# Two unused pads move TensorE's moving buffers by 32 bytes in SBUF

## The chip, the core and the metric

The kernel runs on one core of one Trainium2 chip, as a single launch. The metric is the device time of one execution in microseconds (us); lower is better. All weights and activations are float32.

## What is computed

The reference is two transformer stacks in a row on 256 tokens of width 1024. The first has two layers, each FFN, mixer, FFN; the second has one layer, mixer and FFN. Every FFN is a SwiGLU of inner width 2816, and makes up most of the work:

```python
def swiglu(h, w_gate, w_up, w_down):
    return (jax.nn.silu(h @ w_gate) * (h @ w_up)) @ w_down

for layer in range(DEPTH):                       # DEPTH = 2
    x = x + 0.5 * swiglu(rms_norm(x, ffn1_norm[layer]), ...)
    h = rms_norm(x, mix_norm[layer])
    x = x + even_mixer(h, ...)  if layer % 2 == 0 else  x + odd_mixer(h, ...)
    x = x + 0.5 * swiglu(rms_norm(x, ffn2_norm[layer]), ...)
x = rms_norm(x, final_norm)
...
# second block, one layer, 16 meta tokens ahead of the 256
h = h + concat([mla_mixer, diff_mixer, swa_mixer]) @ w_out
h = h + (silu(hn @ w_gate) * (hn @ w_up)) @ w_down
```

The mixers are attentions (a global and a windowed one, a neighbourhood one, and three kinds in the second block), each with an input projection and an output projection.

## The kernel before, in words

**The weights.** All large weight matrices pass through a ring of six slots, one block of 128 x 1024 numbers in each. SyncE loads a block into `w_raw` (`load`). ScalarE rounds it to the float32r format in `w_hi` (line 914), and VectorE writes the rest, `w_raw - w_hi`, to `w_lo` (line 1371). The activations are split in the same way. A product is then three matmuls at full rate: high with high, high with low, low with high.

**The transposed activations.** `act_t` holds the normed activations with the feature on the partition: for each of 8 feature tiles k, 256 columns of high parts and 256 of low parts. ScalarE writes the high parts (line 935), VectorE the low ones (line 1412), at each norm. `hid_t` holds three tiles of the FFN's inner activations in the same form (ScalarE at line 992, VectorE at line 1525). `out_t` and `hid_t`, and the last three tiles of `act_t`, hold the attention outputs for the output projections (`out_pair`).

**The matmuls.** A matmul has a stationary operand, loaded by LDWEIGHTS, and a moving operand, which streams past it. Each matmul here has a weight load of its own. The page prints the moving operand first in the list of inputs: `gu<-sb_act_t,sb_w_hi` has `act_t` moving and a 128 x 128 piece of `w_hi` stationary.

- `gate_up` (line 2054), first tiles in `first_tile` (2021) and `opening_tile` (2031, 2035): `act_t` moves, 512 columns (high and low at once) against `w_hi`, then 256 against `w_lo`.
- `cols_block` (line 2066) and `last_cols` (line 2108): the down product of the first four FFNs. `hid_t` moves, 256 columns, in groups of three: `w_hi`, `w_hi`, `w_lo`.
- `half_block` (line 2089) and again `last_cols` (2108): the output projections. `hid_t`, `out_t` and tiles of `act_t` move, 256 columns each, by the same code.
- the chunks at lines 2294, 2439 and 2557: queries and keys, `act_t` moves, 256 columns.
- the other projections (lines 2232, 2263, 2523) and the down product of the last FFN (2127, 2134, 2146): the weights move and `act_t` or `hid_t` is stationary.

The stretch that the change touches is the list of buffers; the order in which these calls get their memory sets the addresses:

```python
        w_raw = sb("w_raw", [P, RING, BLK])
        w_hi = sb("w_hi", [P, RING, BLK], F32R)
        w_lo = sb("w_lo", [P, RING, BLK], F32R)

        act_t = sb("act_t", [P, KT, 2 * SEQ], F32R)
        meta_t = sb("meta_t", [P, KT * 4 * META + META], F32R)
        hid_t = sb("hid_t", [P, 3, 2, SEQ], F32R)
        out_t = sb("out_t", [P, 2, 2 * SEQ], F32R)
        x = sb("x", [P, KT, SEQ])
```

and the two places that most matmuls come from are

```python
                            ins = nc.tensor.matmul(gu[:, b, w, 0:width], part[:, s, cols], act_t[:, k, 0:width],
                                                   start=(k == 0 and i == 0), stop=(k == KT - 1 and i == 1))
```

```python
                        for i, (part, rhs) in enumerate(((w_hi, rhs_hi), (w_hi, rhs_lo), (w_lo, rhs_hi))):
                            ins = nc.tensor.matmul(y[:, b, c * SEQ:(c + 1) * SEQ], part[:, s, cols], rhs,
                                                   start=(first and c == 0 and i == 0), stop=False, skip_group_check=True)
```

**Addresses.** The buffers lie one behind the other in each partition. In the built program `w_raw` starts at byte 16512, and the sizes in the list give the rest. What matters below is the address modulo 128 bytes, called the phase here. All offsets inside `w_hi`, `w_lo` and `act_t` that matmuls use are multiples of 128 bytes, and those inside `hid_t` and `out_t` are multiples of 1024, so each buffer has one phase:

| buffer | byte before | phase before | byte after | phase after |
|---|---|---|---|---|
| w_raw, w_hi, w_lo | 16512, 41088, 65664 | 0 | the same | 0 |
| act_t | 90240 | 0 | 90272 | 32 |
| meta_t | 106624 | 0 | 106656 | 32 |
| hid_t | 108736 | 64 | 108768 | 96 |
| out_t | 114880 | 64 | 114912 | 96 |
| x and all that follows | 118976 | 64 (x) | 119104 | the same as before |

Of the kernel before, what the change touches and what calls it, by code (L numbers as in the profile page):

```python
# [21 lines left out]
P = 128  # L22
# [261 lines left out]
def build(nc, a, out):  # L284

    ctx = ExitStack()
    with ctx:
        def sb(name, shape, dt=F32):
            return ctx.enter_context(nc.sbuf_tensor("sb_" + name, shape, dt))
# [6 lines left out]
        w_hi = sb("w_hi", [P, RING, BLK], F32R)  # L296
        w_lo = sb("w_lo", [P, RING, BLK], F32R)

        act_t = sb("act_t", [P, KT, 2 * SEQ], F32R)
        meta_t = sb("meta_t", [P, KT * 4 * META + META], F32R)  # L300
        hid_t = sb("hid_t", [P, 3, 2, SEQ], F32R)
        out_t = sb("out_t", [P, 2, 2 * SEQ], F32R)
        x = sb("x", [P, KT, SEQ])
        work = sb("work", [P, TT, WORK])
        mwork = sb("mwork", [P, MWORK])
# [2493 lines left out]
```

## Time and profile before

| | |
|---|---|
| median of 3 runs | 1295.4 us (1294.29 to 1295.53) |
| the profiled execution | span 1298.1 us; no other time is recorded for it |
| TensorE matmul busy | 1274.0 us, 98% of the span |
| VectorE, ScalarE, GpSimd busy | 77%, 57%, 11% |
| mean DMA rate | 180 GB/s |
| mean granted TensorE clock | 0.996 |

The span runs from the first to the last instruction. It is 2.7 us over the median of the timed runs. Matmuls overlap each other in the profile, since each is shown with its way through the array; the pace is read from their starts.

### The profile page before, as it was taken

The page shows a single profiled execution, that of the slowest core. Times are in us where ns is not written, and L with a number is a line of the kernel's source. Part 1 is how long each engine was busy: PE and PEld are TensorE (multiplying, and loading weights), DVE is VectorE, ACT ScalarE, POOL GpSimd, SP SyncE. Part 2 cuts the span into 40 slices and gives each one's busy share as a digit, 9 for nine tenths or more (in the row PEclk, how much of TensorE's full clock was granted, in tenths as well). Part 3 has the DMA queues.
Part 4 walks back from the last instruction along what each step waited for, and adds up shares of the span by engine and source line. Part 5 has one row for each costly group of instructions (what it writes and reads, how often), then busy time and mean ns, then how long its engine had stood idle before and what let it go on. Part 6 is the DMA issues. An engine that isn't in the chain of part 4 may idle for free.

```text
span 1298.1 us, 24356 instructions
## 1 busy us (share of the span) xinstructions
PE 1274.0 (98%) x8455; PEld 1135.3 (87%) x8455; DVE 994.7 (77%) x1863; ACT 736.5 (57%) x1331; POOL 142.1 (11%) x229
## 2 busy tenths in 40 slices
PE   7999999999999999999999999999999999999997
PEld 6899999788899998999988889999998868888886
DVE  6877778968887778777786758877777677877775
ACT  6555556766555556555555556555556655655553
POOL 5000003202330000000002202000005410000000
PEclk9999999999999999999999999999999989999999
DMA  9866655537996647665649537666657412666650
GB/s 283 258 186 193 184 188 147 154 117 198 268 258 189 194 147 219 185 185 186 194 141 263 171 108 231 213 184 188 194 153 183 134 46 82 204 185 193 183 172 33
DMA packets 295612, 233.57 MB, mean 180 GB/s; under 512 B 13180, under 2 KB 270532, under 8 KB 295552
## 3 DMA queue, kind: packets, MB, share of 16 engines
q1 hardware_dynamic: 288432, 213.80, 55.2%
q0 software_dynamic: 6688, 18.60, 5.8%
q8 instruction: 38, 0.62, 0.2%
q10 hardware_dynamic: 432, 0.36, 0.1%
q14 instruction: 22, 0.18, 0.1%
HBM read 229.79 MB, written 7.55 MB: 183 GB/s over the span
## 4 chain that ended last, share of the span: by engine, by line
PE 89%; DVE 5%; DMA 2%; ACT 2%; issue 1%; POOL 0%; SPq 0%; POOLq 0%; DVEq 0%; ACTq 0%
PE gu L2054 42%; PE y L2066 16%; PE y L2146 4%; PE gu L2439 4%; PE y L2108 3%; PE gu L2263 2%; PE y L2089 2%; PE gu L2089 2%; PE gu L2232 2%; DVE sb_w_lo L1371 2%; PE gu L2021 1%; DMA sb_w_raw<-in_ffn_w_up 1%; PE y L2477 1%; PE gu L2454 1%; PE y L2466 1%; PE gu L2294 1%
## 5 line engine op out<-in xcount | busy, mean ns | idle before, releaser
L2054 PE MATMUL gu<-sb_act_t,sb_w_hi 128*128 128x512 f32 x1680 | 587.9, 394 | 0.0
L1371 DVE TENSOR_TENSOR sb_w_lo<-sb_w_raw,sb_w_hi 128x1024 fp32r<-128x1024 f32 (+1 forms) x405 | 496.0, 1229 | 89.8 <-ACT sb_w_hi L914 83.5
L914 ACT ACTIVATE sb_w_hi<-sb_w_raw 128x1024 fp32r<-128x1024 f32 (+1 forms) x405 | 423.9, 1052 | 70.8 <-PE y L2066 30.7
L2054 PE MATMUL gu<-sb_act_t,sb_w_lo 128*128 128x256 f32 x1680 | 434.7, 279 | 0.0
L2054 PEld LDWEIGHTS gu<-sb_act_t,sb_w_hi 128*128 128x128 f32 x1680 | 307.4, 188 | 55.3
L2054 PEld LDWEIGHTS gu<-sb_act_t,sb_w_lo 128*128 128x128 f32 x1680 | 316.1, 188 | 14.9
L2066 PE MATMUL y<-sb_hid_t,sb_w_hi 128*128 128x256 f32 x1216 | 218.7, 280 | 3.5 <-DVE sb_hid_t L1525 3.5
L980 ACT ACTIVATE sb_work<-gu 128x256 f32<-128x256 f32 x220 | 84.0, 382 | 237.1 <-PE gu L2054 230.8
L2066 PEld LDWEIGHTS y<-sb_hid_t,sb_w_hi 128*128 128x128 f32 x1216 | 190.5, 188 | 7.8 <-DVE sb_w_lo L1371 2.9
L2066 PE MATMUL y<-sb_hid_t,sb_w_lo 128*128 128x256 f32 x608 | 170.2, 280 | 0.0
L1504 DVE TENSOR_TENSOR sb_work<-gu,sb_work 128x256 f32<-128x256 f32 x220 | 92.6, 423 | 96.4 <-ACT sb_work L980 96.4
L2066 PEld LDWEIGHTS y<-sb_hid_t,sb_w_lo 128*128 128x128 f32 x608 | 114.1, 188 | 0.0
L1508 DVE TENSOR_TENSOR sb_work<-sb_work 128x256 f32<-128x256 f32 x220 | 94.5, 431 | 8.4 <-ACT sb_work L1001 1.2
L992 ACT ACTIVATE sb_hid_t<-sb_work 128x256 fp32r<-128x256 f32 x110 | 46.0, 418 | 80.3 <-DVE sb_work L1519 80.3
L643 POOL TENSOR_TENSOR sb_small<-sb_small 128x2 f32<-128x2 f32 (+3 forms) x16 | 19.4, 1212 | 465.9 <-DVE sb_small L1459 461.7
L985 ACT ACTIVATE sb_work<-sb_work 128x256 f32<-128x256 f32 x110 | 46.0, 418 | 24.5 <-DVE sb_work L1508 24.0
L1519 DVE SCALAR_TENSOR_TENSOR sb_work<-sb_work 128x256 f32<-128x256 f32 x110 | 47.0, 427 | 11.1
L1525 DVE TENSOR_TENSOR sb_hid_t<-sb_work,sb_hid_t 128x256 fp32r<-128x256 f32 x110 | 46.8, 425 | 5.3 <-ACT sb_hid_t L992 5.3
L1060 ACT ACTIVATE sb_prob<-sb_prob,sb_small 128x256 f32<-128x256 f32 (+1 forms) x88 | 42.0, 482 | 14.9 <-DVE sb_small L1810 10.4
L1513 DVE SCALAR_TENSOR_TENSOR sb_work<-sb_work 128x256 f32<-128x256 f32 x110 | 46.7, 425 | 3.2 <-ACT sb_work L985 2.4
L1074 ACT ACTIVATE sb_prob_t<-y 128x512 f32<-128x512 f32 (+1 forms) x42 | 23.2, 587 | 45.3 <-PE y L2466 33.2
L2439 PE MATMUL gu<-sb_act_t,sb_w_hi 128*128 128x256 f32 x256 | 47.6, 287 | 0.0
(357 smaller groups left out, 1649.4 us busy)
## 6 DMA issues: line engine op xcount, KB each, us to landing
sb_w_raw<-in_ffn_w_gate SPq DMA_DIRECT2D x88, 512.0 KB, 3.8
sb_w_raw<-in_ffn_w_up SPq DMA_DIRECT2D x88, 512.0 KB, 3.7
sb_w_raw<-in_ffn_w_down SPq DMA_DIRECT2D x88, 512.0 KB, 3.3
sb_w_raw<-in_odd_w_qkv SPq DMA_DIRECT2D x24, 512.0 KB, 6.6
sb_w_raw<-in_w_gate SPq DMA_DIRECT2D x22, 512.0 KB, 3.8
sb_w_raw<-in_w_up SPq DMA_DIRECT2D x22, 512.0 KB, 3.7
sb_w_raw<-in_w_down SPq DMA_DIRECT2D x22, 512.0 KB, 3.6
sb_w_raw<-in_even_w_in SPq DMA_DIRECT2D x12, 512.0 KB, 3.8
```

What stands on the lines that cost most here:

```text
L914: nc.scalar.activation(w_hi[:, slot, 0:w], w_raw[:, slot, 0:w], ACT.Copy).then_inc(hi_done, 1)
L980: nc.scalar.activation(halves[:, b, w, :], gu[:, b, w, SEQ:2 * SEQ], ACT.Copy).then_inc(half_copied, 1)
L1371: nc.vector.tensor_tensor(w_lo[:, slot, 0:w], w_raw[:, slot, 0:w], w_hi[:, slot, 0:w].bitcast(F32), ALU.subtract).then_inc(lo_done, 1)
L1504: nc.vector.tensor_tensor(sums[:, b, w, :], gu[:, b, w, 0:SEQ], halves[:, b, w, :], ALU.add).then_inc(gu_summed, 1)
L1508: nc.vector.tensor_tensor(sums[:, b, w, :], sums[:, b, w, :], rstd_row, ALU.mult).then_inc(scaled, 1)
L1519: nc.vector.scalar_tensor_tensor(out=hidden[:, b, :], in0=gated[:, b, :], scalar=0.5, in1=sums[:, b, 1, :], op0=ALU.mult, op1=ALU.mult).th ...
L1525: nc.vector.tensor_tensor(hid_t[:, h, 1, :], hidden[:, b, :], hid_t[:, h, 0, :].bitcast(F32), ALU.subtract).then_inc(hidden_split, 1)
L2054: ins = nc.tensor.matmul(gu[:, b, w, 0:width], part[:, s, cols], act_t[:, k, 0:width], start=(k == 0 and i == 0), stop=(k == KT - 1 and i ...
L2066: ins = nc.tensor.matmul(y[:, b, c * SEQ:(c + 1) * SEQ], part[:, s, cols], rhs, start=(first and c == 0 and i == 0), stop=False, skip_grou ...
L2089: ins = nc.tensor.matmul(mixed(kind, b)[:, c * SEQ:(c + 1) * SEQ], part[:, s, cols], rhs, start=(at == 0 and c == 0 and i == 0), stop=Fals ...
L2146: ins = nc.tensor.matmul(y[:, 2 * t + h, :], lhs[:, tok], part[:, s, h * 512:(h + 1) * 512], start=False, stop=False, skip_group_check=True)
L2439: ins = nc.tensor.matmul(gu[:, c % 2, 1, 0:SEQ], part[:, s, cols], rhs, start=(k == 0 and i == 0), stop=(k == KT - 1 and i == 2))
```

## The change

Two tensors that nothing reads or writes are allocated: 32 bytes per partition ahead of `act_t`, and 96 bytes behind `out_t`. `act_t`, `meta_t`, `hid_t` and `out_t` move up by 32 bytes; everything behind them moves up by 128 bytes, and so keeps its address modulo 128. The weights stay. Every instruction is the same, in the same order and with the same waits; only line numbers grow, by 1 from `act_t` on and by 2 from `x` on (line 2054 becomes 2056).

```diff
         w_hi = sb("w_hi", [P, RING, BLK], F32R)
         w_lo = sb("w_lo", [P, RING, BLK], F32R)
 
+        phase_a = sb("phase_a", [P, 8])
         act_t = sb("act_t", [P, KT, 2 * SEQ], F32R)
         meta_t = sb("meta_t", [P, KT * 4 * META + META], F32R)
         hid_t = sb("hid_t", [P, 3, 2, SEQ], F32R)
         out_t = sb("out_t", [P, 2, 2 * SEQ], F32R)
+        phase_b = sb("phase_b", [P, 24])
         x = sb("x", [P, KT, SEQ])
         work = sb("work", [P, TT, WORK])
         mwork = sb("mwork", [P, MWORK])
```

## Rows read from the trace of the kernel before

**Rows 1.** The page: span, busy time by engine, clock granted in 40 slices.

```profile
span 1298.1 us, 24356 instructions
PE 1274.0 (98%) x8455; PEld 1135.3 (87%) x8455; DVE 994.7 (77%) x1863; ACT 736.5 (57%) x1331; POOL 142.1 (11%) x229
...
PEclk9999999999999999999999999999999989999999
```

**Rows 2.** Waits of PE: who was waited for, us in total, times, longest.

```profile
PE gu L1981 <- DMA sb_gain_rows<-in_ffn_norm: 5.8, 1, 5.8
PE y L2066 <- DVE sb_hid_t L1525: 3.5, 3, 1.2
```

**Rows 3.** Groups of PE by shape: count, then busy us, mean ns, idle before.

```profile
L2054 PE MATMUL gu<-sb_act_t,sb_w_hi 128*128 128x512 f32 x1680 | 587.9, 394 | 0.0
L2054 PE MATMUL gu<-sb_act_t,sb_w_lo 128*128 128x256 f32 x1680 | 434.7, 279 | 0.0
L2066 PE MATMUL y<-sb_hid_t,sb_w_hi 128*128 128x256 f32 x1216 | 218.7, 280 | 3.5 <-DVE sb_hid_t L1525 3.5
L2066 PE MATMUL y<-sb_hid_t,sb_w_lo 128*128 128x256 f32 x608 | 170.2, 280 | 0.0
L2439 PE MATMUL gu<-sb_act_t,sb_w_hi 128*128 128x256 f32 x256 | 47.6, 287 | 0.0
```

**Rows 4.** Line 2108 alone, four stretches: length, PE busy (count), PEld, clock, DMA share.

```profile
191.07:199.55 8.48, 8.48 (x72) 8.43 (x71) 1.00 0.55 161
288.08:293.84 5.76, 5.76 (x48) 5.72 (x48) 1.00 1.01 308
473.85:482.33 8.48, 8.48 (x72) 8.43 (x71) 1.00 0.44 137
780.46:786.22 5.76, 5.76 (x48) 5.72 (x48) 1.00 1.07 311
```

**Rows 5.** Line 2108: duration ns min/median/max by operand.

```profile
L2108 PEld LDWEIGHTS y<-sb_hid_t,sb_w_hi x192: 187/188/189, 190.8 to 971.7; 128*128 128x128 f32 x192
L2108 PE MATMUL y<-sb_hid_t,sb_w_hi x192: 278/279/280, 191.1 to 971.8; 128*128 128x256 f32 x192
...
L2108 PEld LDWEIGHTS y<-sb_act_t,sb_w_hi x48: 192/192/192, 290.8 to 1102.1; 128*128 128x128 f32 x48
L2108 PE MATMUL y<-sb_act_t,sb_w_hi x48: 283/283/283, 291.0 to 1102.2; 128*128 128x256 f32 x48
```

**Rows 6.** Line 2066 alone, in a stretch of full DMA.

```profile
314.41:317.24 2.83, 2.83 (x24) 2.78 (x23) 1.00 1.00 288
```

**Rows 7.** Timeline of PE in a gate and up product: start us, us.

```profile
312.67 0.39 PE L2054 MATMUL gu<-sb_act_t,sb_w_hi 128*128 128x512 f32 x1
312.90 0.28 PE L2054 MATMUL gu<-sb_act_t,sb_w_lo 128*128 128x256 f32 x1
...
313.71 0.39 PE L2054 MATMUL gu<-sb_act_t,sb_w_hi 128*128 128x512 f32 x1
```

**Rows 8.** Timeline of PE, the moving operand a weight: line 2232, then 2146.

```profile
669.61 0.62 PE L2232 MATMUL gu<-sb_w_hi,sb_act_t 128*128 128x512 f32 x2
...
674.38 0.61 PE L2232 MATMUL gu<-sb_w_hi,sb_act_t 128*128 128x512 f32 x2
...
1141.62 0.63 PE L2146 MATMUL y<-sb_w_hi,sb_hid_t 128*128 128x512 f32 x2
1142.09 0.63 PE L2146 MATMUL y<-sb_w_lo,sb_hid_t 128*128 128x512 f32 x2
1142.56 0.39 PE L2146 MATMUL y<-sb_w_hi,sb_hid_t 128*128 128x512 f32 x1
```

**Rows 9.** Line 2414 alone, matmuls of 256 columns of plain float32.

```profile
1048.94:1051.95 3.01, 3.01 (x15) 2.47 (x13) 1.00 0.61 180
```

**Rows 10.** Stretches, all engines: PE, PEld, DVE, ACT, POOL, clock, DMA share, GB/s.

```profile
300.00:360.00 60.00, 57.76 (x381) 52.31 (x381) 49.09 (x77) 32.51 (x54) 21.84 (x30) 1.00 0.98 257
640.00:700.00 60.00, 60.00 (x375) 53.95 (x373) 42.03 (x62) 34.04 (x51) 6.29 (x9) 1.00 0.69 184
```

## The prediction

> **What bounds the kernel now.** I read the page first. TensorE's matmuls are busy for 1274.0 of 1298.1 us, and its clock is at full rate in all slices but one, which is just under [rows 1]. Then the waits of PE: the largest are 5.8 us at the very start and 3.5 us in three pieces [rows 2]. So the kernel is a queue of 8455 matmuls on one engine, and the time is their number times the pace at which they start. A change of pace goes into the time almost one to one. The groups say which matmuls count: 3360 at line 2054 with `act_t` moving and 1824 at line 2066 with `hid_t` moving [rows 3].
>
> Next I asked what the pace is made of. The granted clock of 1.00 is 2.4 GHz, so 256 columns at one a cycle take 106.7 ns and 512 take 213.3. In the gate and up product three pairs of 512 and 256 columns start between 312.67 and 313.71, which is 347 ns a pair against 320.0 [rows 7]: 27 ns too much, or 13.3 a matmul. That excess does not grow with the width: with weights moving, 21 matmuls of 512 columns start between 669.61 and 674.38, 227 ns each, 13.8 over 213.3 [rows 8]. It is a fixed price per matmul, paid nearly everywhere.
>
> **Is an address able to change it?** The trace holds an experiment on this by itself. Line 2108 is one piece of code, run with `hid_t` moving (phase 64) and with `act_t` moving (phase 0); the weights are at phase 0 in both. With `hid_t` 72 matmuls take 8.48 us, 117.8 ns each; with `act_t` 48 take 5.76 us, 120.0 each; and each repeats to the digit elsewhere in the program [rows 4]. The instructions themselves are shorter, 279 against 283 ns, and their weight loads 188 against 192, with hardly any spread [rows 5]. The `act_t` stretches fall where the DMA queues are full, 1.01 and 1.07 against 0.55 and 0.44, so I looked for `hid_t` under full DMA: at line 2066, with a share of 1.00, 24 matmuls take 2.83 us, 117.9 each [rows 6]. DMA is not the cause. What is left that differs is the address of the moving operand. A second pair goes the other way: with the weights moving at phase 0, a stationary `act_t` (phase 0) gives 227 ns, and a stationary `hid_t` (phase 64) gives four starts in 0.94 us, 235 ns [rows 8]. These two lines also differ in the order of their outputs, so that is weaker. I conclude that the phase counts, by 2 to 8 ns a matmul, and that no row shows phase 32 or 96.
>
> **The change part by part.** The pads cost no instruction. Nothing is added to any queue, no wait appears, and no order moves.
>
> 1. *`act_t` moving, phase 0 to 32.* The matmuls are 3360 at line 2054, 160 in the first tiles, 384 at 2439, 192 at 2557, 120 at 2294, and 216 in the output projections: 4432 (where no row is shown, the code gives the count: at line 2557 8 chunks of 8 feature tiles by 3). Unknown price. From below (a gain): the whole excess but that of line 2414, where 14 matmuls start in 3.01 us, 215 ns each for 256 columns of plain float32 [rows 9]; at two cycles a column that is 213.3, so 1.7 ns is left as excess, and the gain could be 11.6 ns each. From above (a loss): the 8 ns of [rows 8]. Between these I take the nearest row, the same line with a moving operand off phase 0 [rows 4]: 120.0 to 117.8, a gain of 2.2 ns. 4432 x 2.2 = 9.8 us.
> 2. *`hid_t` and `out_t` moving, phase 64 to 96.* 1824 at line 2066, 288 at 2108, 360 at 2089: 2472. These are off phase 0 before and after. I take 117.8 ns for both, a change of 0. The bounds: back to 120.0 costs 2472 x 2.2 = 5.4 us; down to 1.7 of excess gains 9.4 ns each, 23 us.
> 3. *`act_t` and `hid_t` stationary, to 32 and 96.* 336 and 264 matmuls. Bounds: minus 264 x 8 = 2.1 us if `hid_t` leaves what makes 235, plus 336 x 8 = 2.7 us if `act_t` enters it. I take 0.
> 4. *Writers of the moved buffers, and everything behind them.* ScalarE and VectorE are at 57 and 77% [rows 1]; a few ns on a write are covered by matmuls in flight. What lies behind keeps its phase. 0. If the cover is gone the engine waits as in rows 2, a few us.
> 5. *What a faster TensorE meets.* In the stretch from 300 to 360 us the DMA share is 0.98 and PE already idles for 2.2 us; in the stretch from 640 it does not idle at all and the share is 0.69 [rows 10]. In the first a gain is given back: 381 of 8455 matmuls, 4.5% of 9.8, is 0.4 us. Next late would be the weight blocks there.
>
> Sum: -9.8 + 0 + 0 + 0.4 = -9.4 us. Against the profiled span that is 1298.1 to 1288.7; the median lies 2.7 below that span, so 1295.4 - 9.4 = 1286.0 us.
>
> The Trainium skill, page "TensorE: Matmul & The Clock Gate", section "Back-to-back issue gap", gives a warm gap of N/2.4 plus 2.5 ns. The plain float32 row comes near that rule and the float32r rows do not. By the rule as a floor that both phases reach, the sum would be near the larger-gain rival below.
>
> **The rivals.**
>
> *A larger gain.* The excess is a clash of two streams that start together from addresses of equal phase, and the new phases take most of it away. For: plain float32 shows that this engine can run with 1.7 ns. Against: phase 64 against 0 was already a different phase, and cured only a sixth. All of it would give -4432 x 11.6 - 2472 x 9.4 = -75 us, 1221; a third of it 1271.
>
> *No change.* The step from phase 0 to 64 helps, but 32 behaves as 0 and 96 as 64, because the memory is organised in pieces of 64 bytes or the buffers differ by something else. 1295.4.
>
> The Trainium skill, page "SBUF — State Buffer", section "Specifications (TRN2)", puts the line of SBUF at 16 bytes. Phases 0, 32, 64 and 96 all begin such a line, so by that rule alone the time would stay. Rows 4 show two such starts that differ, so the rule is not all there is.
>
> *Slower.* A start at 32 or 96 lies across a boundary of 64 bytes, while 0 and 64 lie on one. Every touched stream then reads one piece more. A row gives the size such an effect can have, 8 ns [rows 8]: 6904 moving matmuls x 8 = 55 us, 1351. If only the small difference appears and on the wrong buffers, 2472 x 2.2 = 5.4 us, 1300.8. It decides from 0.4 ns a matmul on: 6904 x 0.38 = 2.6 us. For: no row shows a start off 64 bytes. Against: the two phases that I can see do not rank the way a simple alignment would have it, since 64 is faster than 0.
>
> **How the numbers follow.** A measurement of this kernel can tell 0.2%, 2.6 us, from no change. The forecast (a gain of 2.6 to 20 us) gets 0.37, with its own range of 1276 to 1292; a larger gain 0.15; no change 0.13; slower 0.35, most of it up to 1322 (4 ns on each moving matmul is 27 us) and 0.13 beyond. So faster is 0.52, same 0.13, slower 0.35. The range leaves out the top 0.13 and some 0.07 of the larger gain: 1262 to 1322.
>
> **What would show it.** In the profile of after, line 2108 becomes 2110. If step 1 is right, its `act_t` stretches fall from 5.76 us per 48 to about 5.65, and the pair in the gate and up product from 347 ns to about 343. If step 2 is right, its `hid_t` stretches stay at 8.48 us per 72. Step 3 is read from the weights-moving lines, 227 and 235 ns; step 5 from the idle time in the 300 to 360 stretch. A pair above 348 ns would make the forecast wrong, whatever the rest shows; a pair under 335 would make the larger gain right.

## The result, and the profile after

| | before | changed |
|---|---|---|
| median | 1297.6 us (1294.29 to 1300.4, 13 runs) | 1300.4 us (1298.3 to 1302.57, 13 runs) |
| span of the profiled execution | 1298.1 us | 1296.5 us |

The ratio is 1.0023, with a 95% interval of 1.0012 to 1.0034: the change makes the kernel about 3 us slower. The forecast was 9.4 us faster. Ten more runs of before put its median at 1297.6, 2 us above the three that the prediction had.

The profiled executions stand the other way round, so their spans have to be cleared of chance first. Here is the page of the changed kernel, then its largest waits of PE.

```profile
span 1296.5 us, 24356 instructions
...
PE 1274.5 (98%) x8455; PEld 1138.0 (88%) x8455; DVE 993.9 (77%) x1863; ACT 735.8 (57%) x1331; POOL 142.3 (11%) x229
...
PEclk9999999999999999999999999999999999999999
```

```profile
PE gu L1983 <- DMA sb_gain_rows<-in_ffn_norm: 5.3, 1, 5.3
...
PE y L2068 <- DVE sb_hid_t L1527: 1.1, 1, 1.1
```

The clock row has no dip, where [rows 1] has one. The stretch with that dip, before and then changed (the number after the counts is the granted clock):

```profile
960.00:1110.00 150.00, 145.86 (x1024) 121.78 (x1022) 109.03 (x296) 87.54 (x220) 38.28 (x57) 0.98 0.38 107
```

```profile
960.00:1110.00 150.00, 145.84 (x1040) 122.03 (x1039) 111.12 (x301) 88.35 (x222) 39.25 (x58) 1.00 0.40 110
```

A clock 0.02 lower over 150 us is some 3 us (an estimate from these two rows) that the profiled execution of before lost, and the two waits shown took 9.3 us there [rows 2] and 6.4 here. What remains is the pace of the matmuls, and it can be read without either. Line 2108 is now 2110; the same four stretches as [rows 4]:

```profile
191.23:199.86 8.63, 8.63 (x72) 8.58 (x71) 1.00 0.54 161
288.26:293.91 5.65, 5.65 (x48) 5.60 (x48) 1.00 1.09 324
473.47:482.11 8.64, 8.64 (x72) 8.58 (x71) 1.00 0.46 144
781.15:786.80 5.65, 5.65 (x48) 5.61 (x48) 1.00 1.11 324
```

`act_t` moving has gone from 120.0 to 117.7 ns a matmul, as forecast. `hid_t` moving has gone from 117.8 to 119.9, where I had 0. Now the two products that make up most of the program. First a gate and up product of 16 pairs (line 2054, now 2056) in the FFN's loop, before and then changed; then the down product behind it (line 2066, now 2068), before and then changed:

```profile
45.58:51.14 5.56, 5.56 (x32) 4.75 (x32) 1.00 0.91 277
```

```profile
44.82:50.39 5.57, 5.57 (x32) 4.78 (x32) 1.00 0.97 287
```

```profile
51.14:53.97 2.83, 2.83 (x24) 2.78 (x23) 1.00 0.60 192
```

```profile
50.39:53.27 2.88, 2.88 (x24) 2.82 (x23) 1.00 0.60 190
```

The gate and up product is where I had put 7.4 of the 9.8 us of gain. Here it did not move: 348 ns a pair both times. In the last FFN it did. There the blocks of 16 pairs alternate between two lengths before, 5.56 and 5.64 us, and all take 5.57 in the changed kernel; the longer kind before, then the same place in the changed kernel:

```profile
1186.40:1192.04 5.64, 5.64 (x32) 4.79 (x31) 1.00 0.65 203
```

```profile
1185.18:1190.75 5.57, 5.57 (x32) 4.78 (x31) 1.00 0.74 211
```

Averaged over the four FFNs before it, a pair went from 348.1 to 348.6 ns; in the last it went from 350.4 to 348.3. The two cancel. The down product of the loop takes 0.05 us more for 24 matmuls. The weights-moving line 2232 (now 2234), with `act_t` stationary, has become slower too, against 227 ns in [rows 8]:

```profile
669.81 0.63 PE L2234 MATMUL gu<-sb_w_hi,sb_act_t 128*128 128x512 f32 x2
...
673.31 0.63 PE L2234 MATMUL gu<-sb_w_hi,sb_act_t 128*128 128x512 f32 x2
```

That is 15 matmuls in 3.50 us, 233 ns each.

**The ledger.** For every line below, and every matmul shape in it, I took the times between successive matmul starts in the trace, replaced those over 1.15 times their median (a wait, a break or a lowered clock lies there) by the mean of the rest, and added them up. Changed minus before, in us:

| matmuls | forecast | changed - before |
|---|---|---|
| gate and up, lines 2054 and 2021, `act_t` moving | -7.7 | -0.3 |
| 256 columns of `act_t`: 2439, 2557, 2294, 2108, 2089 | -2.0 | -2.3 |
| `hid_t`, `out_t` moving: 2066, 2108, 2089 | 0 | +5.1 |
| weights moving: 2232, 2263, 2523, 2127, 2146 | 0 | +0.9 |
| sum | -9.7 | +3.4 |

The forecast's -9.8 has 32 more matmuls, those of the opening tile. The timed runs say +3.0 (0.23% of 1297.6). So the ledger holds the change, and is used below. The lines left out are small matmuls of the attentions, broken up by waits; with them the sum of a version changes by some 1 us either way.

### The profile page after: what moved, and what is told of

It is laid out like the page before. It is cut to its first block, busy times and chain, and to the rows that moved or that the text cites. A ratio compares the mean times of both kernels' runs of the same rounds, so it can differ in the third digit from the quotient of the medians.

```text
span 1296.5 us, 24356 instructions
## 1 busy us (share of the span) xinstructions
PE 1274.5 (98%) x8455; PEld 1138.0 (88%) x8455; DVE 993.9 (77%) x1863; ACT 735.8 (57%) x1331; POOL 142.3 (11%) x229
## 4 chain that ended last, share of the span: by engine, by line
PE 90%; DVE 5%; ACT 2%; DMA 2%; issue 1%; POOL 0%; POOLq 0%; SPq 0%; ACTq 0%; DVEq 0%
PE gu L2056 43%; PE y L2068 16%; PE y L2148 4%; PE gu L2441 3%; PE y L2110 2%; PE gu L2265 2%; PE y L2091 2%; PE gu L2091 2%; PE gu L2234 2%; DVE sb_w_lo L1373 1%; DMA sb_w_raw<-in_ffn_w_up 1%; PE y L2479 1%; PE gu L2456 1%; PE y L2468 1%; PE gu L2296 1%
## 5 line engine op out<-in xcount | busy, mean ns | idle before, releaser
L2068 PE MATMUL y<-sb_hid_t,sb_w_hi 128*128 128x256 f32 x1216 | 221.8, 281 | 1.1 <-DVE sb_hid_t L1527 1.1
```

## The experiments

All are the kernel before with pads of other sizes. The diffs are against the kernel before; lines of the list that do not change are left out or shortened to `...`. Two numbers name a version: the distance of `act_t` and of `hid_t` (`out_t` has the same) from the weights `w_hi` and `w_lo`, in bytes modulo 256. Before is (0, 64), the changed kernel (32, 96). The labels have other numbers: they count modulo 128 up to the fourth run and from the fifth on modulo 256, so that `a32_h64` is (32, 192). The ratio is to the kernel before on the same chip.

**`a32_h64`: (32, 192), only act_t leaves its phase modulo 128.**

```diff
+        phase_a = sb("phase_a", [P, 8])
         act_t = ...
         meta_t = ...
+        phase_h = sb("phase_h", [P, 24])
         hid_t = ...
```

> Only act_t and meta_t move to phase 32; hid_t and out_t keep phase 64. Theory A (each moving buffer has a pace of its own, set by its phase): the act_t matmuls of 256 columns go from 120.0 to 117.4 ns as in the changed kernel, the pairs at the gate and up product stay at 348.6, hid_t stays at 117.8; 912 x -2.6 ns and 96 x +6 ns make -1.8 us, ratio 0.9986. Theory B (the loss comes from the shift of everything behind by 128 bytes, or from act_t): at or above the changed kernel, +2.8 us, ratio 1.002.

Measured: 1287.1 us, ratio 0.9899 (0.9882 to 0.9917). By the medians this is 11 us faster, six times the gain that theory A allowed, and theory B allowed none. Line 2108 (2110 here):

```profile
189.18:197.35 8.17, 8.17 (x72) 8.12 (x71) 1.00 0.58 164
285.11:290.71 5.60, 5.60 (x48) 5.56 (x48) 1.00 1.00 307
```

`act_t` is at 116.7 ns, but `hid_t`, which I thought to have left alone, is at 113.5. Modulo 128 it is where it was; modulo 256 it is not. So the period is longer than 128 bytes. It also means that no version here moves `act_t` alone to 32: (32, 64) was never run.

**`a0_h96`: (0, 96), only hid_t and out_t move.**

```diff
         meta_t = ...
+        phase_h = sb("phase_h", [P, 8])
         hid_t = ...
         out_t = ...
+        phase_b = sb("phase_b", [P, 24])
```

> Only hid_t and out_t move, to phase 96. Theory A: hid_t and out_t go from 117.8 to 119.8 ns, 2472 x 2.05 = +5.1 us, ratio 1.0039; act_t stays at 120.0 and 348.6 per pair. Theory B: between 1.000 and 1.002, with hid_t at 117.8.

Measured: 1305.8 us, ratio 1.0059 (1.0042 to 1.0075). The 32 bytes on `hid_t` and `out_t` are what costs time. Line 2108, then the gate and up product in the loop:

```profile
191.51:200.15 8.64, 8.64 (x72) 8.59 (x71) 1.00 0.56 162
288.91:294.67 5.76, 5.76 (x48) 5.71 (x48) 1.00 0.96 305
```

```profile
44.59:50.19 5.60, 5.60 (x32) 4.77 (x32) 1.00 1.01 302
```

`hid_t` goes to 120.0 and `act_t` stays at 120.0 here. But the gate and up product takes 5.60 us against 5.56, though nothing in it has moved. Over the program that is +3.6 us in the ledger, beside +5.3 from `hid_t` and `out_t`. So a product's pace can depend on something besides the distances of its own operands. It may be the matmuls that ran before it, or the writes into `hid_t` while it runs. The last FFN speaks for the first: there `hid_t` is written as elsewhere but is stationary in the product before, and a pair takes 350.2 ns against 350.4. That is an argument from one case, no test.

**`all32`: (0, 64), the weights move too.**

```diff
+        phase_w = sb("phase_w", [P, 8])
         w_raw = ...
...
         out_t = ...
+        phase_b = sb("phase_b", [P, 24])
```

> Weights too move by 32 bytes (phase 32), act_t 32, hid_t 96: all distances between the operands of a matmul are as before. Theory C (what counts is the distance between the moving and the stationary address): the paces of before, 120.0 and 117.8 ns, ratio 1.000. Theory D (what counts is the moving operand's own phase, as in a start across a boundary): 117.4 and 119.8 ns as in the changed kernel, ratio 1.002.

Measured: 1298.6 us, ratio 1.0004 (0.9990 to 1.0018). Every pace is that of before, to 0.6 ns a matmul, and the ledger has +0.0. A start across a boundary of 64 bytes costs nothing: here every operand has one.

```profile
191.02:199.50 8.48, 8.48 (x72) 8.43 (x71) 1.00 0.57 164
288.03:293.79 5.76, 5.76 (x48) 5.72 (x48) 1.00 1.00 301
```

**`same128`: (128, 192).** One pad of 128 bytes ahead of `act_t`.

> 128 bytes ahead of act_t: every buffer behind the weights moves by 128 bytes, all phases modulo 128 as before. If 128 bytes is a whole period: 120.0, 117.8 and 348.6 ns, ratio 1.000. If the period is longer: other paces, and a ratio off 1.000; theory B asks for 1.002.

Measured: 1297.8 us, ratio 1.0003 (0.9992 to 1.0014). The time is the same and the paces are not, so 128 is no period: gate and up +2.7 us in the ledger, the down product -1.0, line 2232 at 232.5 ns. The shift of everything behind the pads, which the changed kernel has too, is not what costs. The down product shows something more. Two blocks of 24 matmuls at line 2066 (2067 here), the first and a later one, same instructions and same buffers' distances:

```profile
23.77:26.49 2.72, 2.72 (x24) 2.69 (x24) 1.00 1.15 294
50.00:52.83 2.83, 2.83 (x24) 2.78 (x23) 1.00 0.71 215
```

The first runs at 113.3 ns a matmul, the second at 117.9. In `a32_h64`, with `hid_t` at the very same byte, it is the other way round:

```profile
24.96:27.78 2.82, 2.82 (x24) 2.78 (x24) 1.00 1.17 287
50.69:53.41 2.72, 2.72 (x24) 2.68 (x23) 1.00 0.71 236
```

So at this distance two steady paces exist, and which one a block of 24 takes is not set by the addresses alone. The same holds at distance 64. In the kernel before one of the 76 blocks at line 2066 runs at the fast pace, 21 matmuls in 2.38 us, 113.3 ns each:

```profile
324.48 0.28 PE L2066 MATMUL y<-sb_hid_t,sb_w_lo 128*128 128x256 f32 x1
...
326.86 0.28 PE L2066 MATMUL y<-sb_hid_t,sb_w_lo 128*128 128x256 f32 x1
```

Its neighbours run at 118.0. In `all32` one block is fast, in `same256` (below) two, none of them the block that is fast in before. The distance decides which pace nearly all blocks take: 75 of 76 the slow one at (0, 64), 70 of 76 the slow one at (128, 192), 73 of 76 the fast one at (32, 192).

**`same256`: (0, 64) again.** One pad of 256 bytes ahead of `act_t`.

> 256 bytes ahead of act_t. Distances from here on are the moving buffer's address minus the weights' address, modulo 256: before has act_t at 0 and hid_t at 64, and keeps both here. Theory E (only these distances modulo 256 count, and the run with 128 bytes differed because 128 is half a period): the paces of before to 0.3 ns, 348.6 a pair, 353.8 a group of three at the down product, ratio 1.000. If the period is longer or there is none: other paces.

Measured: 1296.8 us, ratio 0.9993 (0.9977 to 1.0009). All means are those of before; the ledger is 0.0. The pace repeats after 256 bytes and, by `same128`, not after 128.

**`a160_h64`: (160, 64).** Pads of 160 bytes ahead of `act_t`, 96 ahead of `hid_t` and 128 behind `out_t`.

> act_t at distance 160, hid_t at 64. Theory E with a half period that matters only for some buffers: hid_t as before (353.8 a group), act_t chunks of 256 columns near 117. Theory F (the pace of a buffer also depends on the matmuls that ran before it): hid_t's group leaves 353.8 by several ns though its address distance is that of before.

Measured: 1296.7 us, ratio 0.9990 (0.9975 to 1.0006). The group of three at line 2066 stays at 353.3 ns, the chunks go to 117.6 a matmul, the pair to 347.9. Ledger -2.5. Theory F asked for a change of the group here, and there was none. All 76 blocks took the slow pace of distance 64.

**`a64_h192`: (64, 192).** Pads of 64 bytes ahead of `act_t` and 64 ahead of `hid_t`.

> act_t at distance 64, hid_t at 192, where the group of three took 340.7 ns with act_t at 32 and 352.1 with act_t at 128. Theory E (own distance only) can't hold already; theory F gives again another group time than 340.7. For the act_t chunks of 256 columns: hid_t at distance 64 took 117.9 each, so 117.9. Ratio between 0.990 and 1.000.

Measured: 1292.8 us, ratio 0.9963 (0.9949 to 0.9976). The group is at 341.8 ns in the loop, and 353.3 at line 2108, again both paces in one program. The chunks are at 117.8, as forecast from `hid_t` at 64. The pair has gone up to 352.1, +5.9 us in the ledger. This was in no expectation.

**`a32_h160`: (32, 160).** Pads of 32 bytes ahead of `act_t`, 64 ahead of `hid_t` and 32 behind `out_t`.

> act_t at 32 and hid_t at 160, to see whether the gain of the run with 32 and 192 comes from act_t at 32 (then near 0.990 again) or from hid_t at 192 (then the group of three is back near 353 to 360, and the ratio near 1.000). The act_t chunks should stay at 117 each.

Measured: 1301.0 us, ratio 1.0021 (1.0010 to 1.0032). The group is at 359.8, the chunks at 116.9. The gain of (32, 192) is that of `hid_t` at 192.

The profiled executions of this version and of (32, 192) both have a stretch at line 2066 in which the granted clock is 0.50, which is 1.2 GHz. `a32_h160`, then `a32_h64`:

```profile
337.60:339.52 1.92, 1.92 (x11) 1.92 (x11) 0.50 0.96 271
```

```profile
331.23:333.15 1.92, 1.92 (x10) 1.92 (x10) 0.50 1.03 303
```

In each, 9 matmuls start in 1.92 us, 213.3 ns each (the counts in the rows include those in flight at the edges). That is 256 columns at 1.2 GHz with nothing over, at a distance of 160 and of 192; `raw32` shows the same at 64. At full clock the two distances differ by 6.6 ns. So the price per matmul, and its dependence on the distance, show at 2.4 GHz and not in these stretches at 1.2.

**`w224`: (32, 96), the distances of the change made from the other side.**

```diff
         w_raw = ...
+        phase_r = sb("phase_r", [P, 56])
         w_hi = ...
         w_lo = ...
+        phase_a = sb("phase_a", [P, 8])
         act_t = ...
...
+        phase_b = sb("phase_b", [P, 32])
         x = ...
```

> The distances of the changed kernel (act_t 32, hid_t and out_t 96) made in another way: w_hi and w_lo move by 224 bytes, act_t and hid_t by 256, so that these keep their address modulo 256 and the weights leave it. If only distances between TensorE's operands count: 348.6 a pair, 359.5 a group, 350.7 at the chunks, ratio 1.002 as in the changed kernel. If the absolute address of the activations counts: the paces of before, ratio 1.000.

Measured: 1301.0 us, ratio 1.0037 (1.0019 to 1.0056), ledger +3.2 against +3.4 for the changed kernel. Line 2108 (2111 here) has 8.62 and 5.66 where the changed kernel has 8.63 and 5.65:

```profile
191.46:200.08 8.62, 8.62 (x72) 8.58 (x71) 1.00 0.56 163
288.47:294.13 5.66, 5.66 (x48) 5.61 (x48) 1.00 0.96 301
```

`act_t` and `hid_t` lie at their old address modulo 256 here. What counts is their distance to the weights `w_hi` and `w_lo`. In another trace the pace also falls differently on the blocks: `act_t` at line 2108 takes 117.8, 117.8 and 116.7 ns in its three stretches in the changed kernel, and 117.8, 116.7 and 117.8 here.

**`raw32`: (0, 64), only w_raw is off by 96 against the rest.** Pads of 32 bytes ahead of `w_raw` and 96 ahead of `w_hi`.

> w_raw, which TensorE never reads, moves by 32 bytes; w_hi, w_lo and all behind move by 128 together, so every distance between TensorE's operands is that of before, but w_raw lies 96 bytes off against them. Theory G (only TensorE's own two streams, moving and stationary, are involved): the paces of before, 348.6, 353.8 and 359.0 ns. Theory H (the reads and writes of ScalarE and VectorE at the weights' split take part): other paces.

This version ran once, for its paces: 353.9 ns a group, 359.0 at the chunks, 348.7 a pair, all as before. Its single time, 1302.9 us, says nothing on a few us.

```profile
193.99:202.47 8.48, 8.48 (x72) 8.43 (x71) 1.00 0.57 166
290.98:296.74 5.76, 5.76 (x48) 5.71 (x48) 1.00 0.97 294
```

The address of the raw weights, which ScalarE and VectorE read, takes no part. What these engines write into `w_hi` and `w_lo` has the same distance to `hid_t` as TensorE's own weight loads, so addresses cannot tell the two apart. A stretch of before in which neither engine did anything can. It lies in the block of [rows 6]; all engines (the pairs of numbers are PE, PEld, VectorE, ScalarE, GpSimd):

```profile
315.83:317.12 1.29, 1.29 (x13) 1.29 (x12) 0.00 (x0) 0.00 (x0) 0.00 (x0) 1.00 1.04 349
```

The 11 matmuls that start from 315.83 to 317.13 come every 118 ns, as in the rest of the block. So the pace does not need the writes of the other engines.

**`a160_h192`: (160, 192).** Pads of 160 bytes ahead of `act_t` and 224 ahead of `hid_t`.

> act_t at 160, where the pair took least (347.9), hid_t at 192, where its group took least (340.7). If each keeps its best: 1680 x -0.7 and 704 x -13 ns and 1 to 2 us from the rest make -12 us, ratio 0.990. If the group depends on what ran before it, as with act_t at 128: the group at 352 and a ratio near 0.998.

Measured: 1293.7 us, ratio 0.9969 (0.9957 to 0.9982). The pair is at 347.8, but the group is at 352.6, near the slower of its two paces (71 of 76 blocks took it). The parts can't be picked one by one.

**`a32_h224`: (32, 224).** Pads of 32 bytes ahead of `act_t`, 128 ahead of `hid_t` and 96 behind `out_t`.

> hid_t 32 bytes beyond its best distance, at 224, with act_t at 32. A smooth dependence would put the group of three near 345 ns and the ratio near 0.993; a narrow one puts it at 354 to 360 and the ratio at 1.000 to 1.003.

Measured: 1298.7 us, ratio 1.0006 (0.9984 to 1.0028). The group is at 354.5: the dependence is narrow, not smooth. 32 bytes away from 192, none of the 76 blocks takes the fast pace.

All of it in one table: nanoseconds for a pair at line 2054, a group of three at 2066 and at 2439, and three matmuls at 2232 (means over the line, waits left out), the ledger and the timed change.

| (act_t, hid_t) | pair 2054 | three 2066 | three 2439 | three 2232 | ledger us | ratio |
|---|---|---|---|---|---|---|
| (0, 64) before | 348.6 | 353.8 | 359.0 | 681.8 | 0 | 1 |
| (0, 64) same256 | 348.6 | 353.6 | 359.0 | 681.8 | 0.0 | 0.9993 |
| (0, 64) all32 | 348.6 | 353.7 | 358.8 | 683.4 | 0.0 | 1.0004 |
| (32, 96) changed | 348.6 | 359.5 | 350.7 | 699.6 | +3.4 | 1.0023 |
| (32, 96) w224 | 348.6 | 359.6 | 350.0 | 699.9 | +3.2 | 1.0037 |
| (0, 96) | 350.7 | 359.8 | 359.2 | 681.4 | +9.1 | 1.0059 |
| (32, 160) | 348.4 | 359.8 | 350.7 | 699.2 | +2.6 | 1.0021 |
| (32, 192) | 349.1 | 340.7 | 350.7 | 699.7 | -12.2 | 0.9899 |
| (32, 224) | 349.0 | 354.5 | 350.2 | 700.2 | -0.4 | 1.0006 |
| (64, 192) | 352.1 | 341.8 | 353.3 | 699.7 | -4.7 | 0.9963 |
| (128, 192) | 350.2 | 352.1 | 358.2 | 697.4 | -0.4 | 1.0003 |
| (160, 64) | 347.9 | 353.3 | 352.7 | 699.8 | -2.5 | 0.9990 |
| (160, 192) | 347.8 | 352.6 | 353.5 | 700.4 | -4.6 | 0.9969 |

The ledger and the timed ratio agree within 1.7 us in every row.

## Why the prediction was wrong

**What bounds the kernel: right.** In every version the timed change is the change of TensorE's pace, to within 1.7 us.

**That an address can change the pace: right, but not which one.** I took the moving operand's phase modulo 128 as the cause. `all32` and `w224` show that it is the distance between the moving and the stationary operand, and `same128` and `same256` that it counts modulo 256. In the trace of before the weights lie at phase 0 throughout, so phase and distance are the same number there and it could not tell them apart. It also had `hid_t` blocks at 117.9 and one at 113.3 ns, which one phase, one pace does not allow.

**Step 1, the gain at `act_t`: the step that failed in size.** The 2.2 ns came from line 2108, where every matmul has 256 columns, and there and at the chunks the size was right: the forecast was -2.0 us, the ledger has -2.3. That fit is partly luck, since the price was taken from `hid_t` at 64 with a cause that does not hold, and another distance of `act_t`, 128, gives only 0.3 ns a matmul at line 2439. I used it for the 3360 matmuls of the gate and up product too, where 512 and 256 columns take turns. There the price of the change was 0.0 ns over the program, +0.6 a pair in four FFNs and -2.1 in the last. [Rows 7] had shown a different rhythm, and I took its excess of 13.3 ns a matmul to be the same thing because the number was the same. It is a mean of two unlike numbers: over the line the next start came 232.0 ns after a matmul of 512 columns and 116.5 after one of 256, which is 18.7 and 9.8 over the columns. Nor is it a fixed price, since it is gone at the lower clock. The text had said that a pair above 348 ns would make the forecast wrong, and the mean was 348.6, as before. That alone leaves 2.6 of the 9.8 us: 2.3 at the 256 columns and 0.3 in the first tiles of the gate and up product.

**Step 2, `hid_t` at no change: the step that failed in sign.** I took 117.8 ns for phase 96 because phase 96 is off phase 0 as 64 is. It measured 119.8 to 120.0; the upper bound of the text, 5.4 us, is nearly what the ledger has, 5.1. Without this loss the change would still have been a small gain; with it the sum is a loss. `a0_h96`, which moves these two buffers alone, shows it by itself.

**Step 3, stationary operands: 0 against a bound of 2.7.** The ledger has +0.9, most of it from line 2232, 227 to 233 ns. That `act_t` would enter what makes `hid_t` slow there is what the row shows; that `hid_t` would leave it was wrong (line 2146 at 233 ns before, 234 after). The bound of 8 ns came from four starts; over the whole line 2146 took 233, so 6 ns was the distance.

**Steps 4 and 5.** Nothing there could be seen: the 300 to 360 us stretch idled 2.2 us before [rows 10] and 1.1 after, and the waits for `hid_t` at this line differ as much among the other profiles (3.5 us before, 2.7 in `same128`, 1.3 in `a0_h96`).

**The rivals.** *Slower* came true with its smallest price and place, "the small difference appears on the wrong buffers", given as 1300.8 us from a base of 1295.4. That 1300.4 was measured is partly chance: the base was 2.2 us higher, and `act_t` gave 2.6 us back. The mechanism given for its large price, one more piece read across a boundary of 64 bytes, is refuted by `all32`. *No change* by lines of 16 bytes is refuted: all versions start on such a line and the time goes from 1287 to 1306. The Trainium skill's page "SBUF — State Buffer", section "Specifications (TRN2)", gives lines of 16 bytes. The Trainium skill's page "TensorE: Matmul & The Clock Gate", section "Step-by-step: what each phase is for" of Part 2, calls the two read ports of TensorE independent and says that loading weights takes no read bandwidth from the running matmul. In the runs here the pace does depend on how the two operands lie to each other (113.4 to 120.0 ns), which that statement would not lead one to expect; whether read bandwidth is what is shared, no run shows. *A larger gain* exists, 11 us at (32, 192), but not at the distances of this change, and the 1.7 ns over the columns that the rival allowed was reached nowhere: the least is 6.7, 113.4 against 106.7.

**What stays open.** That the two streams of TensorE disturb each other fits all of it, but no run shows where they meet. What is shown is that the distance modulo 256 changes the pace, and not that it alone sets it. Which part of the path makes the price vanish at 1.2 GHz is open too. Why the alternating pairs hardly react to `act_t` at 32 and lose 5.9 us at 64 is open. So is what selects one of the two paces of a block. Equal bytes and unequal paces within one program show that it is not the addresses alone; that it is the way in which the block begins is a guess. A wait ahead does not decide it: the first block of `same256` and that of `raw32` both begin with a pause (193 and 195 ns to the second start), and run at 113.3 and at 117.9.

## What to carry to other kernels

Where TensorE is the bound and each matmul loads its own weights, the relative address of the moving and the stationary buffer was worth 1.5% between the best and the worst version here, and costs only a pad to try. Move one buffer at a time and measure each combination, because the effects of two need not add up: the pair at line 2054 takes 350.7 ns with only `hid_t` moved to 96, and 348.6 with `act_t` moved too. Read the pace from starts of matmuls in stretches without waits: the mean over a line repeats to some 0.1 ns a matmul (353.8, 353.6 and 353.7 ns for three in the versions with equal distances), where the 13 timed runs of before span 0.5%. Look at single blocks too, since a mean can hide two paces. And a price measured on one rhythm of matmuls (256, 256, 256 columns) must not be carried to another (512, 256), even when both show the same excess.

## What the runs showed of the hardware

- The pace of float32r matmuls, each with a weight load of its own, depends on the distance between the operands' addresses modulo 256 bytes: with 256 columns moving, 113.4 to 120.0 ns, against an estimate of 106.7 ns for the columns alone (256 at one a cycle of 2.4 GHz). Moving all operands together by 32 bytes, or the activations by 256, changes nothing.
- At a granted clock of 0.50 the same matmuls started every 213.3 ns at distances of 64, 160 and 192, which is 256 columns at 1.2 GHz with nothing over.
- At one distance the same instructions ran at two steady paces, block by block in the same program: 113.4 and 117.7 ns at 192, 113.3 and 117.9 at 64.
- The pace of a product can change when only buffers move that it does not read (5.56 to 5.60 us per 32 matmuls in `a0_h96`, where `hid_t` and `out_t` moved).
- The distances of `act_t` that help where it moves with 256 columns (32, 64 and 160: 350 to 354 ns for three at line 2439, against 359.0) hurt where it is stationary and 512 columns of a weight move: line 2232 went from 227 to 233 ns in every version with `act_t` off distance 0.
